# Segment sums of the even mixer as products of one fixed triangle, and cross attention's heads turned in pairs

## What is computed

```python
cums = jnp.cumsum(dt * a, axis=2)
seg = cums[:, :, :, None] - cums[:, :, None, :]
lmat = jnp.exp(jnp.where(causal, seg, -jnp.inf))
```

```python
s = jnp.einsum('bshd,bmhd->bhsm', q, k) * (XATTN_HEAD_DIM ** -0.5)
p = jax.nn.softmax(s, axis=-1)
o = jnp.einsum('bhsm,bmhd->bshd', p, v).reshape(bsz, seq, -1)
return o @ wo
```

## Time and profile before

| | us |
|---|---|
| median of three runs | 1201.73 |
| lowest, highest | 1201.43, 1202.47 |
| profiled execution, its own time | 1201.93 |
| its span, first to last instruction | 1200.0 |
| TensorE busy | 1191.0 |
| VectorE busy | 793.0 |
| ScalarE busy | 642.0 |
| POOL busy | 121.8 |

### The profile page before, as it was taken

One profiled execution on the slowest core, in us unless ns is written; L12 is line 12 of the kernel. 1 busy time (PEld: TensorE's weight loads), 2 busy tenths in 40 slices (PEclk: granted clock), 3 DMA queues, 4 the chain that ended last, 5 costly groups with the idle time before them and its releaser, 6 DMA issues.

```text
span 1200.0 us, 17666 instructions
## 1 busy us (share of the span) xinstructions
PE 1191.0 (99%) x7001; PEld 1045.8 (87%) x7001; DVE 793.0 (66%) x841; ACT 642.0 (53%) x871; POOL 121.8 (10%) x105
## 2 busy tenths in 40 slices
PE   9999999999999999999999999999999999999997
PEld 8888889889989888888888888899988898888886
DVE  6766766865657676656676656677786676666664
ACT  7554546553556554444465444454676565544443
POOL 1000001640142020000020000020012122000001
PEclk9999999999999999999999999999999999999999
DMA  9966655544444465656556556555623425665560
GB/s 319 338 206 187 199 179 172 164 157 142 140 157 156 141 211 185 200 177 205 177 175 194 191 183 202 178 162 187 211 102 110 147 100 176 228 192 193 182 203 35
DMA packets 164880, 214.75 MB, mean 179 GB/s; under 512 B 14816, under 2 KB 140896, under 8 KB 164704
## 3 DMA queue, kind: packets, MB, share of 16 engines
q1 hardware_dynamic: 164544, 213.30, 54.7%
q0 software_dynamic: 144, 0.52, 0.1%
q10 hardware_dynamic: 144, 0.26, 0.1%
HBM read 213.02 MB, written 1.05 MB: 178 GB/s over the span
## 4 chain that ended last, share of the span: by engine, by line
PE 95%; DMA 2%; DVE 1%; ACT 1%; issue 0%; POOL 0%; SPq 0%; POOLq 0%; DVEq 0%
PE ps L2012 29%; PE ps L1991 15%; PE ps L2019 15%; PE ps L1992 15%; PE ps L1993 15%; PE ps L2076 1%; DMA raw<-in_ffn_w_down 1%; DMA raw<-in_first_up 1%; ACT xn L1175 1%; PE ps L2531 0%; PE ps L2620 0%; PE ps L2658 0%; PE ps L2681 0%; PE ps L2287 0%; PE ps L2139 0%
## 5 line engine op out<-in xcount | busy, mean ns | idle before, releaser
L2012 PE MATMUL ps<-hT,w_hi 128*128 128x512 f32 x1568 | 374.8, 391 | 0.7 <-DVE hT L1283 0.5
L2012 PEld LDWEIGHTS ps<-hT,w_hi 128*128 128x128 f32 x1568 | 289.9, 188 | 58.8 <-DVE hT L1283 0.7
L1398 DVE TENSOR_TENSOR w_lo<-raw,w_hi 128x2048 fp32r<-128x2048 f32 x108 | 247.6, 2292 | 61.5 <-ACT w_hi L831 61.5
L1243 DVE TENSOR_TENSOR w_lo<-raw,w_hi 128x2048 fp32r<-128x2048 f32 x85 | 195.2, 2306 | 72.3 <-ACT w_hi L701 72.3
L701 ACT ACTIVATE w_hi<-raw 128x2048 fp32r<-128x2048 f32 x85 | 162.2, 1914 | 87.3 <-PE ps L1993 85.8
L2019 PEld LDWEIGHTS ps<-hT,w_lo 128*128 128x128 f32 x1568 | 201.5, 191 | 8.0
L831 ACT ACTIVATE w_hi<-raw 128x2048 fp32r<-128x2048 f32 x108 | 205.8, 1906 | 0.5 <-DMA raw<-in_ffn_w_gate 0.5
L2019 PE MATMUL ps<-hT,w_lo 128*128 128x256 f32 x1568 | 204.0, 283 | 0.0
L1991 PE MATMUL ps<-w_hi,arena_r 128*128 128x512 f32 x354 | 138.4, 391 | 0.2 <-DVE arena_r L1391 0.2
L1992 PE MATMUL ps<-w_lo,arena_r 128*128 128x512 f32 x354 | 137.8, 389 | 0.0
L1993 PE MATMUL ps<-w_hi,arena_r 128*128 128x512 f32 x354 | 137.4, 388 | 0.0
(11 more groups left out here) (320 smaller groups left out, 1629.9 us busy)
## 6 DMA issues: line engine op xcount, KB each, us to landing
raw<-in_ffn_w_down SPq DMA_DIRECT2D x44, 1024.0 KB, 4.8
raw<-in_ffn_w_gate SPq DMA_DIRECT2D x43, 1024.0 KB, 5.3
raw<-in_ffn_w_up SPq DMA_DIRECT2D x43, 1024.0 KB, 5.3
raw<-in_xattn_wkv SPq DMA_DIRECT2D x16, 1024.0 KB, 5.5
raw<-in_even_w_in SPq DMA_DIRECT2D x13, 1024.0 KB, 5.1
raw<-in_xattn_wq SPq DMA_DIRECT2D x8, 1024.0 KB, 5.2
raw<-in_xattn_wo SPq DMA_DIRECT2D x8, 1024.0 KB, 4.9
raw<-in_odd_w_in SPq DMA_DIRECT2D x6, 1024.0 KB, 5.7
```

The lines of the kernel that those rows point to most:

```text
L1243: ins = V.tensor_tensor(lo, src, hi.bitcast(F32), ALU.subtract)
L1398: V.tensor_tensor(w_lo[:, m % RING, :], raw[:, m % RING, :], w_hi[:, m % RING, :].bitcast(F32), ALU.subtract).then_inc(lo_done, 1)
L2012: mm(ps[:, bank0 + m, :], cols(w_hi, n, k, CW, m * P, (m + 1) * P), hT[:, k, :, :].rearrange("p a c -> p (a c)"), start=k == 0, stop=False)
```

## The change

1. POOL no longer scales "after". It multiplies the constant "upto", repeated four times, by four heads' columns of dta, each broadcast over 128 columns: one tensor-tensor instruction of 512 columns for four heads. dta is split in a high and a low part so that the products can be fp32r; that makes eight such instructions (four for each part), into upto_hi (over xk) and upto_lo (over xv), and one subtraction of 16 columns ahead of them. dta's high part is a ScalarE copy, placed after the third third of the convolution has been started and ahead of the next high half of weights. POOL's first instruction now waits for that copy (dta_done 2) instead of dta itself.
2. TensorE makes the segment sums as eight fp32r products of 512 columns (two a bank, high and low part), with one stationary triangle after_r, an fp32r copy of "after" made once by ScalarE in the tenth turn of the first SwiGLU.
3. In both cross attentions turned(0) and turned(1) stand together, as do turned(2) and turned(3), and values(2), values(3) come behind the first wo chunk. ScalarE's and VectorE's queues follow: the outputs of heads 0 and 1 are split ahead of turned heads 2 and 3, and VectorE makes the second wo chunk's low half ahead of head 2's output.

```diff
         small_parts = sb("small_parts", [P, LINES(2 * SMALL_W + 80)], F32R)
+        dta_parts = small_parts[:, 2 * SMALL_W + 80:2 * SMALL_W + 112].rearrange("p (i c) -> p i c", i=2)
+        after_r = sb("after_r", [P, P], F32R)
...
-            ld = xk[:, :, :].rearrange("p k c -> p (k c)").rearrange("p (t h s) -> p t h s", t=TT, h=SSM_H)
+            upto_hi = xk_parts[:, :, :].rearrange("p k c -> p (k c)").rearrange("p (t h s) -> p t h s", t=TT, h=SSM_H)
+            upto_lo = xv_parts[:, :, :].rearrange("p t (h s) -> p t h s", h=SSM_H)
...
                 probs_out(u, 0)
+                probs_out(u, 1)
                 exponentials(2)
-                probs_out(u, 1)
                 exponentials(3)
+                heads_out(0)
+                heads_out(1)
                 probs_out(u, 2)
-                heads_out(0)
                 probs_out(u, 3)
-                for h in range(1, XH):
-                    heads_out(h)
+                heads_out(2)
+                heads_out(3)
                 hi_upto(wq + 7)
...
                     ins.then_inc(es["act_read"], 1)
+                    if c == 2:
+                        act.wait_ge(es["dta_done"], 1)
+                        nc.scalar.activation(dta_parts[:, 0, :], ev.dta, ACT.Copy).then_inc(es["dta_done"], 1)
                     hi_upto(E + c + 4)
...
                 elif c == 1:
+                    nc.scalar.activation(after_r[:, :], const("after"), ACT.Copy)
                     nc.scalar.activation(masks[:, :], masks_f, ACT.Copy).then_inc(consts_made, 1)
...
                 turned_lo(0)
+                turned_lo(1)
                 maxima(3)
                 probabilities(2)
-                turned_lo(1)
                 probabilities(3)
+                b = OT_BASE[f"cross{layer}"]
+                oT_lo(b + 1, 0, 0)
+                oT_lo(b + 2, 2, 1)
                 turned_lo(2)
                 turned_lo(3)
-                for h in range(XH):
-                    oT_lo(OT_BASE[f"cross{layer}"] + h + 1, 2 * h, h)
+                lo_upto(wo + 2)
+                oT_lo(b + 3, 4, 2)
+                oT_lo(b + 4, 6, 3)
                 add_residual(wo + 3, 1.0, ("norm", layer, 3))
...
-            def seg_weights(t):
-
-                pool.wait_ge(es["dta_done"], 1)
-                for h in range(SSM_H):
-                    G.tensor_scalar(ev.ld[:, t, h, :], const("after"),
-                                    ev.dta[:, 8 * t + h:8 * t + h + 1], None, ALU.mult).then_inc(es["ld_done"], 1)
+            def seg_weights():
+
+                pool.wait_ge(es["dta_done"], 2)
+                dta_hi, dta_lo = (dta_parts[:, i, :].bitcast(F32) for i in range(2))
+                step(G.tensor_tensor(dta_parts[:, 1, :], ev.dta, dta_hi, ALU.subtract))
+                upto = const("upto").unsqueeze(1).to_broadcast([P, 4, P])
+                for q in range(4):
+                    for dst, src in ((ev.upto_hi, dta_hi), (ev.upto_lo, dta_lo)):
+                        ins = G.tensor_tensor(dst[:, q // 2, 4 * (q % 2):4 * (q % 2) + 4, :], upto,
+                                              src[:, 4 * q:4 * q + 4].unsqueeze(2).to_broadcast([P, 4, P]), ALU.mult)
+                    ins.then_inc(es["ld_done"], 1)
...
                 turned(0)
+                turned(1)
                 scores(3)
-                turned(1)
                 values(0)
+                values(1)
                 turned(2)
-                values(1)
                 turned(3)
-                values(2)
-                values(3)
                 b = OT_BASE[f"cross{layer}"]
                 key = ("norm", layer, 3)
-                out_chunks(wo, lambda i: pe.wait_ge(oT_done, b + i + 1),
-                           between=turn_ahead(norm_no(layer, 3), key), order=turn_order(key))
+
+                def head_ready(i):
+                    if i == 1:
+                        values(2)
+                        values(3)
+                    pe.wait_ge(oT_done, b + i + 1)
+
+                out_chunks(wo, head_ready, between=turn_ahead(norm_no(layer, 3), key), order=turn_order(key))
...
                 for q in range(4):
-                    pe.wait_ge(es["ld_done"], 4 * q + 4)
+                    pe.wait_ge(es["ld_done"], q + 1)
...
-                    for h in range(4):
-                        last = mm(ps[:, 4 + q, h * P:(h + 1) * P], ev.ld[:, q // 2, 4 * (q % 2) + h, :],
-                                  const("upto"), start=True, stop=True)
+                    for i, part_ in enumerate((ev.upto_hi, ev.upto_lo)):
+                        last = mm(ps[:, 4 + q, :], after_r[:, :],
+                                  part_[:, q // 2, 4 * (q % 2):4 * (q % 2) + 4, :].rearrange("p h s -> p (h s)"),
+                                  start=i == 0, stop=i == 1)
                     last.then_inc(es["seg_mm"], 1)
```

More of the change, by code:

```diff
@@ L1921, in even @@
                 G.memset(ev.xpad[:, :, 0:CONV_W - 1], 0.0).then_inc(es["xpad_zero"], 1)
-                seg_weights(0)
-                seg_weights(1)
+                seg_weights()
                 for i in range(4):
```

## The result

The changed kernel takes **1204.81 us** (median of 10 runs, 1204.62 to 1205.53), the kernel before, measured beside it, 1201.69 us (10 runs, 1201.43 to 1202.47). The ratio is 1.0026 with a 95% interval of 1.0017 to 1.0035: slower by 3.1 us, where 0.3 us had been forecast. The profiled execution took 1205.49 us at a span of 1203.6 us; against the one of before (1201.93 us at 1200.0) the spans differ by 3.6 us. This execution is one of the two long ones: two of the ten have spans of 1203.6 and 1203.7 us, the eight others 1202.6 to 1202.9.

A forecast was written before the change was run, and what follows sets the result against it. TensorE was taken to bound the kernel, busy 1191.0 of 1200.0 us. The terms -1.8 + 2.6 - 0.5 = +0.3 on 1201.73 gave 1202.0 us, own range 1200.6 to 1203.4.

The forecast's parts named there:

- Segment sums, -1.8: TensorE's segment sums: eight fp32r products replace 32 fp32 records, 3.88 us to 2.14; gain 1.8 us, bounds 1.5 to 1.9.
- POOL and VectorE, +2.6: POOL's longer products and VectorE's taps and splits block each other; 2.6 us delay reaches TensorE whole, bounds 0.6 to 5.4.
- the pairs run on, and POOL gets gaps only: Convolution taps on VectorE: pairs run together, each of three pairs letting one POOL product of about 0.8 us in.
- Rival D: VectorE's queue ahead of the first rotation: every tap of 225.01 lets one POOL product through, price 5.4, total 1204.8 us; chance 0.12.
- A: The forecast itself: the gain moves into a TensorE stall at 244.93; 1202.0 us, range 1200.6 to 1203.4; chance 0.45.
- A product's price, 1.04 us: Each of POOL's eight 512-column products with a broadcast operand takes 1.04 us, 8.3 us for all.
- the rotations' bank at v0: TensorE's weight load at 244.93 waits for a PSUM bank that VectorE's rotation frees; slack nought, so the delay enters whole.
- 0.5 of it already at the chunk whose split is late: Of the 2.6 us delay, 0.5 reaches TensorE at the chunk whose split, from 230.51, ends 2.6 us late.
- its sign of being wrong: A TensorE wait over 1 us anywhere other than the forecast places makes the prediction wrong.
- Cross attention, -0.5: Turning heads in pairs removes three TensorE waits, 0.59 us, adds 0.33; 0.26 a layer, 0.5 us for two.
- The loss ahead of the first output chunk: Cross attention: the chunk waits for head 0's low half, ready at 389.48, TensorE free at 389.28; 0.23 us lost.
- the cover of the third chunk's split: Cross attention: third output chunk's split moves to 400.5 to 402.8, wanted at 403.2; cover falls from 5 us to 0.4.

The follow-up runs named there:

- experiment 8: Changed kernel with POOL's eight products replaced by eight scalings of the same 512 columns by one column of dta (three of four heads left out): 1204.70 us.
- experiment 4: Changed kernel with the same eight POOL products moved: five behind the last tap, one behind each of the first three rotations: 1200.44 us.
- Experiment 3: Kernel before plus only ScalarE's copy of dta, with POOL's sixteen old scalings waiting for it: 1202.56 us.
- `seg_alone`: Kernel before plus only the segment sums' part of the change, cross attentions in the old order: 1205.69 us.
- experiment 7: Kernel before, nothing of the change; VectorE writes the seventh projection chunk's low half two times more than needed: 1206.40 us.
- experiment 5: Changed kernel with each POOL product of 512 columns cut into two of 256, in the same places: 1201.50 us.
- experiment 9: Changed kernel with four products on VectorE behind its last tap, four on POOL behind the seventh projection chunk's split and first three rotations: 1199.31 us.
- experiment 6: Changed kernel with six POOL products ahead of and beside the taps, the last two moved behind the first two rotations: 1203.41 us.

## Why the prediction was wrong

- **Segment sums, -1.8:** right. The block gained 1.70.
- **POOL and VectorE, +2.6: the term that failed.** In its place stand 5.1 us of delay: 4.17 in the six taps and 0.93 ahead of them. The failed step is "the pairs run on, and POOL gets gaps only", taken from 2.99 us for six taps beside POOL's scalings. The rows read for it had POOL instructions of 128 columns and one operand. Taps alone take 2.71, so those rows already held the collisions, at 0.07 us for each of the four scalings let in (taken one by one, three of the six taps last 0.54 or 0.59 us instead of 0.47). That was read as no exclusion; it was exclusion by a short one. With 512 columns and two operands the same turn costs 0.74. Rival D had the mechanism, every tap lets one product in, and nearly its size (5.4 against the 5.1 measured), and got a chance of 0.12. The Trainium skill, "SBUF — State Buffer", section "Who interferes with whom", calls the shared port pair an exclusive lock, and says of VectorE's 2-port modes that the lock is held for the whole instruction. It has issue order decide who blocks, but no case of two queues that take turns, so it spoke for A and for D alike; the prediction tied it to A alone. The trace agrees that the two exclude each other; in experiment 8 what VectorE waited for was not the whole POOL instruction, but 0.44 of 1.76 us.
- **A product's price, 1.04 us:** right in quiet air (1.04 in experiment 4), 1.22 beside a tap. POOL ended at 232.8, not at 236: while taps wait for it, it is not the one that waits.
- **Where the delay lands.** The prediction had one place, the rotations' bank at v0, and "0.5 of it already at the chunk whose split is late". With 1.8 us of slack at k1 and none at v0, a delay of 5.1 is 3.3 at k1 and 1.8 at v0. The wait of 3.3 us at k1 is also what the prediction named as its sign of being wrong, a TensorE wait over 1 us in another place. Experiment 3 confirms the zero slack at v0 (1.21 in, 1.20 out).
- **The clock was not in the sum, and in the median it cost nothing that can be seen.** Nothing in the sum asked what a stall of some us does to the products behind. In the profiled execution they lost 2.9 us. Without that TensorE would have had to wait at v0 for rotations that were 5.07 us late; its second token tile there starts at 250.88, 5.95 later than 244.93, so the clock cost 0.9. In the trace of `seg_alone` the delay is the same, the clock took 1.6 us, and the wait at v0 covered all of it. The eight executions of the changed kernel that have spans 0.7 to 1.1 us shorter than the two long ones are taken to be of this second kind; that is inferred from spans, no trace of one was kept.
- **The sum again, for the profiled execution:** 5.95 at v0's second token tile is 5.82 at its end, as the kernel before lost 0.11 there on a slow second product. 5.82 - 1.71 - 0.55 and 0.09 in places not followed are the 3.65 of the profiled spans.
- **And for the median:** TensorE had come to k1 0.26 us ahead of the profile of the kernel before, so against its own pace the rotations were 5.07 + 0.26 = 5.33 late. 5.33 - 1.71 - 0.55 = 3.07, and the medians differ by 3.1: the delay of POOL and VectorE, less the two gains, is the whole loss.
- **Cross attention, -0.5:** right, 0.26 a layer forecast, 0.29 and 0.26 measured. The loss ahead of the first output chunk (0.21 for 0.23) and the cover of the third chunk's split (0.6 us for 0.4) came as forecast.
- **The rival's time.** D gave 1204.8 and the measured median is 1204.81. That is partly luck: of its 5.4, the 4.8 for the taps are 0.6 too much and the 0.6 for the splits are 0.3 too little. It put all of it at v0 and had no clock, which changes the time of a long execution only.

## What to carry over

Where POOL and VectorE share a queue of small instructions, count in turns: each VectorE instruction with both inputs in SBUF let at most one of POOL's in here, and paid for the columns and operands that this one read. A short one (0.07 us) hides in a mean of six; before making it longer, compare the group with one that has no POOL work beside it. Then put the work where the engine waits anyway (the 2.5 us for ScalarE) or beside instructions that read PSUM. And a stall of TensorE as long as those seen here may bring the lower clock for the products behind it; that is to be priced only up to where the next wait would have come anyway (nothing in `seg_alone` and experiment 7, 0.9 us in the changed kernel's profile, all of the loss in experiments 5 and 8).

## What the runs showed of the hardware

**The price of a turn by what POOL reads.** For each POOL instruction let in between taps, worked out from the length of six taps less 2.71 us: 0.07 us (128 columns, one operand), 0.32 (256, two), 0.44 (512, one), 0.74 (512, two). By estimate the last three come to 0.6 to 0.9 ns for each element read in a partition; the third differs from the others in its form too, and the first is from taps of which only three were held. VectorE's rotations, with one input from PSUM and one table from SBUF, lost nothing beside a product (four in 1.65 us in experiment 9, as without one in the changed kernel). The Trainium skill says as much ("SBUF — State Buffer", "Who interferes with whom": a VectorE instruction with at most one SBUF input, outside its 2-port modes, doesn't contend); the trace agrees.

**The same wait did and did not bring the lower clock.** Idle of TensorE beyond its step, and what the granted clock did in the profiled runs: 1.2 us, no fall (experiment 3); 1.4 us, no fall (experiment 8, ahead of v0); 1.9 us twice, no fall (experiment 6); 1.9 us, a fall 1.3 us behind the restart (experiment 5); 2.3 us, a fall (experiment 8); 2.7 us, a fall (experiment 7); 3.3 us, a fall 0.8 us behind the restart (`seg_alone`); 3.3 us, a fall before the wait was over (the changed kernel). It lasted for eight or nine products in `seg_alone` and experiments 5, 7 and 8 (1.6 to 1.8 us lost), fourteen in the changed kernel (2.9). So the same wait of 3.3 us, in the same place, was followed by two different losses. Three windows of experiment 5, the wait and the fall behind it:

```profile
244.00:247.00 3.00, 1.22 (x7) 0.68 (x5) 1.72 (x5) 0.00 (x0) 1.17 (x2) 1.00 0.66 185
247.00:250.00 3.00, 3.00 (x10) 2.37 (x11) 2.80 (x3) 0.00 (x0) 2.99 (x2) 0.71 0.43 165
250.00:253.00 3.00, 3.00 (x13) 2.53 (x12) 1.66 (x4) 1.44 (x1) 1.16 (x3) 0.72 0.92 286
```

The times without a profile fit: in experiment 5 the profiled run lies apart by 1.7 us; in experiment 8 four runs lie at 1202.87 to 1202.94 and six at 1204.70 to 1205.25, with the profiled one, which shows the fall, among the six. In experiment 6 three of eleven lie 1.8 us above most others, and the profiled one, without a fall, among the lower. That the upper groups are the runs with a fall is inferred from these three profiles. The mean clock listed with each run points the same way in experiments 5 and 6 (0.997 in the upper groups, 0.998 or 0.999 in the lower) and does not part the groups in experiment 8 (0.998 above, 0.998 to 1.000 below). What decides it for one wait was not found.
